# First attention of a two-block kernel: one head at a time against groups of four heads with 32-row score products

## What is computed

```python
def rope(x, positions):            # half = 32
    return jnp.concatenate([x1 * cos - x2 * sin, x2 * cos + x1 * sin], axis=-1)

scores = jnp.einsum('bcqhgd,bckhd->bchgqk', q, k_band) * (hd ** -0.5)
scores = jnp.where(mask[None, :, None, None], scores, -jnp.inf)
m = jnp.maximum(jnp.max(scores, axis=-1), sink_l)
p = jnp.exp(scores - m[..., None])
denom = jnp.sum(p, axis=-1) + jnp.exp(sink_l - m)
out = jnp.einsum('bchgqk,bckhd->bcqhgd', p, v_band)
out = out / denom.transpose(0, 1, 4, 2, 3)[..., None]
return out.reshape(B, S, Hq * hd).astype(h.dtype) @ w_out
```

## Time and profile before

| | |
|---|---|
| median of three runs | 1099.14 us |
| profiled execution | 1102.06 us (span 1100.3 us) |
| TensorE matmul busy | 1010.5 us, 92% of the span |
| VectorE busy | 590.8 us, 54% |
| ScalarE busy | 502.1 us, 46% |
| mean granted TensorE clock | 0.955 |
| span between the first head's first transpose and the last product of (`aout`,0) | 395.9 to 487.7 us |

### The profile page before, as it was taken

The page is one execution under the profiler, slowest core; times in us unless marked ns, Lnnn a source line. Parts: engine busy times, 40 slices in busy tenths (PEclk is TensorE's granted clock), DMA queues, the critical chain, the costliest instruction groups (busy, mean ns, idle before and its releaser), DMA issues.

```text
span 1100.3 us, 14326 instructions
## 1 busy us (share of the span) xinstructions
PE 1010.5 (92%) x5201; PEld 843.0 (77%) x5201; DVE 590.8 (54%) x1133; ACT 502.1 (46%) x834; POOL 24.4 (2%) x39
## 2 busy tenths in 40 slices
PE   3999898999999788997999999886899999999996
PEld 3976686888887777776888888775898888788875
DVE  4654766453543764347453544465554366565565
ACT  4555444353451665436343443356333444444542
POOL 0013100000000000000000000000000000000000
PEclk9999998999998987689999999988999999999999
DMA  6451145535444231024546455132242233433441
GB/s 247 173 202 38 68 170 192 206 142 224 164 179 152 78 115 39 1 77 164 212 157 229 147 196 201 66 116 96 83 168 77 77 115 122 147 115 120 149 172 39
DMA packets 25188, 149.46 MB, mean 136 GB/s; under 512 B 2960, under 2 KB 3088, under 8 KB 10800
## 3 DMA queue, kind: packets, MB, share of 16 engines
q1 hardware_dynamic: 24464, 146.39, 36.1%
q0 software_dynamic: 672, 2.38, 0.7%
HBM read 147.71 MB, written 1.05 MB: 135 GB/s over the span
## 4 chain that ended last, share of the span: by engine, by line
PE 79%; DVE 8%; ACT 7%; issue 2%; DVEq 2%; DMA 1%; ACTq 0%; SPq 0%
PE bank L414 22%; PE bank L415 22%; PE bank L416 22%; PE bank L473 2%; PE bank L742 1%; PE bank L719 1%; ACT w_hi L1033 1%; DVE w_lo L1464 1%; DVE w_lo L1485 1%; DVEq L1765 1%; PE bank L830 1%; ACT arena L1015 1%; PE bank L637 1%; PE bank L729 1%; PE bank L845 1%
## 5 line engine op out<-in xcount | busy, mean ns | idle before, releaser
L414 PE MATMUL bank<-w_hi,x_hi 128*128 128x512 f32 (+2 forms) x728 | 298.6, 410 | 14.7 <-DVE ffn_nat L1671 9.3
L415 PE MATMUL bank<-w_lo,x_hi 128*128 128x512 f32 (+2 forms) x728 | 289.9, 398 | 0.0
L416 PE MATMUL bank<-w_hi,x_lo 128*128 128x512 f32 (+2 forms) x728 | 287.4, 395 | 0.0
L414 PEld LDWEIGHTS bank<-w_hi,x_hi 128*128 128x128 f32 x728 | 140.1, 192 | 47.4 <-DVE w_lo L1464 10.1
L1404 DVE TENSOR_TENSOR w_lo<-w_raw,w_hi 128x2048 fp32r<-128x2048 f32 x62 | 140.2, 2288 | 60.1 <-ACT w_hi L978 57.4
L416 PEld LDWEIGHTS bank<-w_hi,x_lo 128*128 128x128 f32 x728 | 139.4, 192 | 31.4
L415 PEld LDWEIGHTS bank<-w_lo,x_hi 128*128 128x128 f32 x728 | 139.9, 192 | 25.9
L978 ACT ACTIVATE w_hi<-w_raw 128x2048 fp32r<-128x2048 f32 x60 | 112.9, 1909 | 31.1 <-DMA w_raw<-w_main_dram 26.6
L1485 DVE TENSOR_TENSOR w_lo<-w_raw,w_hi 128x2048 fp32r<-128x2048 f32 x38 | 86.9, 2290 | 54.7 <-ACT w_hi L1033 54.5
L1221 ACT ACTIVATE arena<-arena,small 128x144 f32<-128x144 f32 (+1 forms) x96 | 45.5, 474 | 111.2 <-DVE small L1768 96.7
L1671 DVE SCALAR_TENSOR_TENSOR ffn_nat<-bank,stat,ffn_nat 128x256 f32<-128x256 f32 x44 | 21.1, 483 | 132.5 <-ACT ffn_nat L1141 132.5
(11 more groups left out here) (284 smaller groups left out, 1452.8 us busy)
## 6 DMA issues: line engine op xcount, KB each, us to landing
w_raw<-w_main_dram SPq DMA_DIRECT2D x112, 1024.0 KB, 4.9
s_raw<-w_side_dram SPq DMA_DIRECT2D x51, 512.0 KB, 4.1
h<-x_dram SPq DMA_DIRECT2D x1, 1024.0 KB, 4.9
arena<-rows_dram POOLq DMA_DIRECT2D x2, 512.0 KB, 4.2
out_dram<-arena SPq DMA_DIRECT2D x1, 512.0 KB, 2.7
out_dram<-arena SPq DMA_DIRECT2D x2, 256.0 KB, 2.1
arena<-c_l_dram POOLq DMA_DIRECT2D x1, 384.0 KB, 5.4
arena<-c_b_dram POOLq DMA_DIRECT2D x1, 264.0 KB, 2.9
```

Source lines behind the costliest of these rows:

```text
L414: pe.matmul(out, ah, bh, start=first, stop=False)
L415: pe.matmul(out, ah, bl, start=False, stop=False)
L416: return pe.matmul(out, al, bh, start=False, stop=last)
```

## The change

- **Groups.** The 16 heads are taken in four groups of four. A group has one head of each key/value head; `HEADS` is reordered. Within a tile of 128 partitions lie now the first rotary halves (32 features) of four heads, and in a second tile their second halves. `aqT` is `[group, half, token]`.
- **Scores.** `a_scores(j)` does a group: for each 128 queries and each half, four products of 32 rows, one for each head, in its own 32 partitions and its own bank; the two halves add up in the bank. That is 16 products of 256 columns a group, where four heads had 8.
- **Rotation.** Both halves of a block pair come out in one bank (512 columns). VectorE multiplies by cos and by sin and adds across the two tiles; ScalarE's copies are gone.
- **Value and key projections.** `av` and `ak` are each one bank, and both are made inside the stream of transposes.
- **Order.** Masks, maxima and divisions go by group (`group_masked`, `group_attended`, one division of 512 columns), the sinks' exponentials once a group. ScalarE is three heads ahead of the transposes. Half blocks of the later queries stand between groups; the output's transposes and the first 6 of 8 steps of (`aout`,0) are inside the last group.
- **Meta tokens.** Their normalisation goes into `ffn(0)`, right behind the angles; their transposes behind the last head.

```diff
+NG = 4
-    keys += [("av", r) for r in range(R)] + [("ak", b) for b in range(2)]
-    keys += [("aq", b) for b in range(8)]
+    keys += [("av",), ("ak",)] + [("aq", j) for j in range(NG)]
...
-AQ_RIDERS = (1, 4, 7, 10)
-AOUT_SPLITS = (1, 4)
+A_HALVES = {0: (C_AOUT, 0), 4: (C_AOUT, 1), 9: (C_AOUT + 1, 0)}
...
-        sc_bank, o_bank = (bank[4], bank[3]), (bank[7], bank[2])
+        sc_bank, as_bank = (bank[4], bank[3]), (bank[2], bank[3], bank[4], bank[6])
...
+            def a_scores(j):
+
+                pe.wait_ge(rot_ok, 2 + j)
+                if j:
+                    pe.wait_ge(nm_ok, NG * j)
+                for r in range(R):
+                    for e in range(2):
+                        for g in range(NG):
+                            rows_ = slice(32 * g, 32 * g + 32)
+                            ins = pe.matmul(as_bank[g][:, r * S:(r + 1) * S], aqT[rows_, j, e, r * P:(r + 1) * P],
+                                            akT[rows_, e, :], start=(e == 0), stop=(e == 1))
+                            if (r, e) == (1, 1):
+                                ins.then_inc(sc_ps, 1)
...
+            a_scores(0)
+            a_queries(2, 0, KT // 2)
+            for j in range(NG):
+                n = NG * j
+                a_turn(n)
+                if j:
+                    a_values(n - 1)
+                if j < NG - 1:
+                    a_scores(j + 1)
+                if j < 2:
+                    a_queries(2 + j, (1 - j) * KT // 2, (2 - j) * KT // 2)
+                if j == NG - 1:
+                    a_out_turn(0)
+                    a_out_turn(1)
+                for i in range(1, NG):
+                    a_turn(n + i)
+                    a_values(n + i - 1)
+                    if (j, i) == (1, 1):
+                        a_queries(3, KT // 2, KT)
+                    if j == NG - 1 and i < NG - 1:
+                        for k in (2 * i - 2, 2 * i - 1):
+                            a_out_turn(k + 2)
+                            a_out_tiles(k)
+            a_out_tiles(KT - 4)
+            a_values(NH - 1)
+            a_out_tiles(KT - 3)
+            a_out_turn(KT - 2)
+            a_out_turn(KT - 1)
...
+                if layer == 0:
+                    act.wait_ge(meta_landed, 16)
+                    act.activation(um[0:M, :], hm[0:M, :], ACT.Square, accum_out=stat[0:M, 0:1]).then_inc(ss_ok, 1)
...
+            for n in range(NG - 1):
+                a_exps(n)
+            for n in range(NH):
+                act.wait_ge(pt_ps, n + 1)
+                if n >= 2:
+                    act.wait_ge(o_ps, n - 1)
+                act.activation(a_pt[:, n % 2, :, :], bank[5][:, :].rearrange("p (a b) -> p a b", a=4), ACT.Copy).then_inc(pt_ok, 1)
+                if n + NG - 1 < NH:
+                    a_exps(n + NG - 1)
+                if n in A_HALVES:
+                    c, g = A_HALVES[n]
+                    split_half(c, c % 2, g)
...
                 if layer == 0:
                     angles()
+                    rstd("meta", [(1, D)], rows=M, out=28)
+                    dve.tensor_scalar(um[0:M, :], hm[0:M, :], stat[0:M, 28:29], None, ALU.mult).then_inc(um_ok, 1)
...
+            def rotated(key, out):
+
+                b = acc_in(key)
+                both = b[:, :].rearrange("p (e s) -> p e s", e=2)
+                dve.drain()
+                dve.tensor_tensor(a_cos, both, cos2, ALU.mult)
+                dve.tensor_tensor(a_sin, both, sin2, ALU.mult).then_inc(acc_free[USE[key] % 2], 1)
+                dve.drain()
+                for e in range(2):
+                    ins = dve.tensor_tensor(out[:, e, :], a_cos[:, e, :], a_sin[:, 1 - e, :], ALU.add)
+                ins.then_inc(rot_ok, 1)
...
             ffn(0, x1)
+            rotated(("aq", 0), aqT[:, 0, :, :])
+            for g in range(2):
+                rest_half(C_AQ + 1, (C_AQ + 1) % 2, g)
+            rotated(("aq", 1), aqT[:, 1, :, :])
...
+            group_masked(0)
+            for j in range(NG):
+                if j:
+                    group_attended(j - 1)
+                if j < NG - 1:
+                    group_masked(j + 1)
+                if j < 2:
+                    rest_half(C_AOUT, C_AOUT % 2, j)
+                    rotated(("aq", 2 + j), aqT[:, 2 + j, :, :])
+                elif j == 2:
+                    rest_half(C_AOUT + 1, (C_AOUT + 1) % 2, 0)
+            rest_st("a_out", x_tile(x_hi), x_tile(x_lo), ks=range(4))
+            rest_half(C_AOUT + 1, (C_AOUT + 1) % 2, 1)
+            rest_st("a_out", x_tile(x_hi), x_tile(x_lo), ks=(4, 5))
+            group_attended(NG - 1)
+            rest_st("a_out", x_tile(x_hi), x_tile(x_lo), ks=(6, 7))
```

More of the change, by code:

```diff
@@ L766, in _, with a_out_turn, a_out_tiles @@
-            mixer_out("aout", C_AOUT, "a_out", lambda r, k: a_o[:, r, k * P:(k + 1) * P], {0: NH}, "f1", o_ok)
+            def a_out_turn(k):
+                if k == 0:
+                    pe.wait_ge(nm_ok, NH)
+                if k % 2 == 0:
+                    pe.wait_ge(o_ok, 2 * k + NG)
+                to_stationary("a_out", lambda r, k: a_o[:, r, k * P:(k + 1) * P], None, 0, ks=(k,))
+            def a_out_tiles(k):
+                st_wait("a_out", k)
+                for r in range(R):
+                    part_a(C_AOUT, ("aout", 0, r), r, k, k + 1)
@@ L767, in _ @@
+            a_out_tiles(KT - 4)
[3 more added lines that the diff above has]
+            a_out_turn(KT - 1)
+            pe.wait_ge(um_ok, 1)
+            for k in range(KT):
+                ins = pe.transpose(bank[6][:, k * M:(k + 1) * M], um[0:M, k * P:(k + 1) * P], ident[0:M, 0:M])
+            ins.then_inc(um_ps, 1)
+            a_out_tiles(KT - 2)
+            a_out_tiles(KT - 1)
+            mixer_rest("aout", C_AOUT, "f1")
             ffn(1, "aout")
@@ L1246, in _ @@
+            act.wait_ge(um_g, 1)
+            act.activation(x_hi[:, :, 0:M], m_tmp, ACT.Copy).then_inc(um_hi, 1)
             mixer_out("aout", C_AOUT, "f1", "norm_ffn1")
@@ L1431, in rest_st, with rstd @@
                     ins.then_inc(st_lo_ok, 1)
-            def rstd(name, parts, rows=P, first=0):
+            def rstd(name, parts, rows=P, first=0, out=24):
                 i, n = RMS[name], sum(w for w, _ in parts)
@@ L1450, in rstd @@
                     dve.drain()
-                    dve.scalar_tensor_tensor(out=y if step < 2 else stat[0:rows, 24:24 + n], in0=t, scalar=1.5, in1=y,
+                    dve.scalar_tensor_tensor(out=y if step < 2 else stat[0:rows, out:out + n], in0=t, scalar=1.5, in1=y,
                                              op0=ALU.add, op1=ALU.mult)
@@ L2059, in main_chunks @@
     return np.stack([k_tiles(p).reshape(P, 2, 4 * CH).transpose(1, 0, 2) for p in parts])
-HEADS = [8 * g + j + 4 * e for g in range(2) for j in range(4) for e in range(2)]
+HEADS = [4 * g + j for j in range(NG) for g in range(NG)]
 def side_units(i):
```

257 lines of the change are left out of this document (116 added, 141 removed).

## The result

The changed kernel takes 1062.61 us (median of 4 runs, 1060.24 to 1064.76) against 1099.80 for the kernel before (4 runs, 1098.64 to 1103.35). The ratio is 0.966, 95% interval 0.963 to 0.969: 37 us faster.

What follows compares the result with a forecast made beforehand. TensorE was taken as the bound, much of its head work at half clock. A gain of 23.3 us up to (`aout`,0), plus 2.0 behind it, less 3.3 in `ffn(0)`, made 22.0: from 1099.14 to 1077.1 us, range 1065 to 1090.

Steps and rivals of the forecast that it cites:

- Four side by side: Head scores: four 32-row products run at once, so a group's scores cost 2.1 us at full clock.
- none side by side: slower than before: Rival for the scores: 32-row products run one behind another, 8.5 us a group at full clock; 1101 to 1118, chance 0.05.
- Up to the first transposes: Attention's start: first head's transposes at 391.2 instead of 395.9, fourth mask ends at 393.0, about 3 us idle.
- The work from 393.0 on: TensorE's work from the second group's scores to the last product of (`aout`,0): 49.8 us at full clock.
- The factor 1.515: Head stretch: the old kernel's 91.8 us over 60.6 of full-clock work, for half clock and waits; applied, it gives 75.4 us.
- The first rival, the clock holds: Head stretch: dense halves and output products keep 2.4 GHz except some 7 us at the start; 1067 us, chance 0.12.
- The 4 us for dense products at the end: Last heads: output products fill 3.5 us of idle and should lift the clock earlier; 4 us taken off.
- Third weight half uncovered: Third group: ScalarE's split of a weight half, 1.91 us, lies under no riding products and would cost up to 1.9.
- Behind (`aout`,0): After that block's last product: the next chunk's load starts earlier, so the following transposes move up; 2 us gained.
- `ffn(0)`: First SwiGLU: the meta tokens' chain moved there makes TensorE wait 3.3 us more, a loss.
- Masks bound: Rival for the groups: both later groups' scores also wait 4.0 us for four masks; 1085 us, chance 0.08.

Runs made afterwards that it cites:

- e2: The changed kernel with a group's scores issued two heads at a time instead of four; 1070.76 us, ratio 0.976 to the kernel before.
- e1: The changed kernel with every group's scores issued one head after another, nothing side by side; 1107.05 us, ratio 1.009 to the kernel before.
- e12: The changed kernel with only the third and fourth groups' scores issued one head after another; 1083.23 us, ratio 0.987 to the kernel before.
- e9: The changed kernel plus 51 throwaway full-array products behind the scores of the third and of the fourth group; 1073.85 us, ratio 0.979 to the kernel before.
- e3: The changed kernel with the first six steps of (`aout`,0) moved behind the last head; 1064.42 us, ratio 0.970 to the kernel before.
- e11: The changed kernel with the meta chain later in the first SwiGLU and two weight halves moved; 1051.86 us, ratio 0.961 to the kernel before.
- e8: The changed kernel with the last two query pairs whole before the first head, not in halves between groups; 1067.38 us, ratio 0.976 to the kernel before.
- e13: The changed kernel with 51 throwaway full-array products at each of two places, each piece cut in four by waits; 1074.95 us, ratio 0.983 to the kernel before.
- e4: The changed kernel with the half query block before the first head moved behind the second group's scores; 1068.08 us, ratio 0.973 to the kernel before.

## Why the prediction was too high

- **Four side by side: right.** 2.1 us a group, measured 1.94. e2 gives 4.08 (4.2 by the prices of the text) and e1 11.9 x 0.65 = 7.7 of work at full clock (8.5). The rival "none side by side: slower than before" gave 1101 to 1118; e1 is 1107.
- **Up to the first transposes: right.** 391.2 and 393.0; measured 391.28 and 393.20, though the axis should have carried 3.3 us from `ffn(0)`. It carries 0.46: TensorE's first transposes of this attention start at 360.15, before at 359.69. The rest came back in places that the change does not touch, where this execution had less half clock; from 75 to 79 us the clock was 0.57 before and 1.00 after. So the piece in between took some 0.4 us less than forecast. That the clock would fall in the 3 us of waits here was wrong: the waits are 1.54 and 1.26, the clock 1.00.
- **The work from 393.0 on: right.** 49.8 at full clock forecast, 51.88 x 0.97 = 50.3 measured.
- **The factor 1.515: this step failed.** It carried half clock and waits over from before to a stretch with other work in it. 75.4 less 4 is 71.4 us; it took 54.2, a factor of 1.09. Those 17.2 us are more than the whole miss of 14.5. The changed kernel pays 27.1 us for a low clock when its thin scores run one after another (e1) and 1.7 when they run side by side. Thin scores took 22.5 us before; the change removes two thirds of that time, and the clock with which everything beside them runs goes up. The cause cannot be scaled with the total: e12 adds 12 us of thin work and pays 20.6, e9 adds as much dense work and pays 11.2.
- **The first rival, the clock holds,** had a chance of 0.12. By the prediction's own sign (a mean clock of the head stretch above 0.85; it is 0.97) it is the true one, and its price was too high: 61.5 us for the stretch, since it kept 8.2 of waits and 3.5 for a low clock at the start; measured are 2.3 and 1.6. Of the two reasons it gave, dense output products are not needed (e3). Dense halves between the groups did not have to be there either in e11's stretch of heads alone; taking both pairs out cost time in e8, but there waits came with it. What made the clock hold, the scores side by side, it did not name.
- **The 4 us for dense products at the end: wrong place.** e3 shows nothing clear of noise for where they stand (1.8 by medians).
- **Third weight half uncovered: right.** Up to 1.9 us; ScalarE's timeline in the changed kernel shows the split (L1094) ahead of the copy (L1293) for which TensorE waits 1.82 us, and the only half clock among the heads begins 2 us behind:

```profile
421.42 1.90 ACT L1094 ACTIVATE w_hi<-w_raw 128x2048 fp32r<-128x2048 f32 x1
423.22 0.57 ACT L1293 ACTIVATE arena<-bank 128x512 f32<-128x512 f32 x1
```

- **Behind (`aout`,0): right.** 2.0 forecast; 15.6 us before (487.7 to 503.31), 13.5 after (447.2 to 460.70), 2.1.
- **`ffn(0)`: nearly.** 3.3 forecast, 2.79 measured.
- **Masks bound: no,** only the second group's scores wait for masks (1.26 us), as in the sum; later scores wait 0.2 us in all, for a rotation (L1787).

In all, of 37.2 us by medians 22.0 were forecast. The profiled pair is 41.8 us apart, so 4.6 of its difference is the choice of executions. The gains of work, start and end were right to about 1 us each; the clock was not treated as something that the change sets.

**Open.** Whether it is the few rows, or the kind of operand and the time per row of results, that makes a product thin for the clock was not separated: the fillers of e9 are split products at twice the pace of the plain fp32 scores, and 64-row products alone were not put against 32-row products of equal length. The half-clock pieces outside the heads are not the same in every profile (75 to 79 us above), and the mean clock of one kernel differs between its executions; no run here looked at why. It is part of the spread, 5 us for the changed kernel and up to 16 for the kernel before.

## What to carry to other kernels

Price a stretch as work at full clock plus clock plus waits, and ask of each of the last two what in the stretch causes it before carrying it over: if the change removes the cause, the factor goes too. Score products of 32 rows are worth packing side by side twice over, for their own time and for the clock of the dense work beside them. But give them as many banks as run together, and check that the engines behind them can feed what TensorE now gains, or it waits for those instead: the pairs of 64-row products gained next to nothing here. A change that relies on overlap should be run once without it: here that version was slower than the kernel before.

## What the runs showed of the hardware that was not expected

- Four products of 32 rows in four partition quarters and four banks run side by side in plain fp32: 32 records in 1.94 us, against 4.08 in pairs and 7.7 of work one head after another (11.9 us at a mean clock of 0.65).
- The granted clock fell while the profile has TensorE 98% busy with thin products: 0.61 to 0.76 in e1's four stretches of 32-row products. With 12 us of full-array products added it stayed at 1.00 (e9), with e1's short waits between them too (e13).
- Once down, it stayed down through heads' transposes and values in which the profile has no gap (e12, 440.30 to 455.00, 0.50). Such heads kept a clock of 1.00 where it had not fallen (e11, 414.00 to 424.00).
- A wait of 4.55 us was followed by 6 us at half clock (e4), and a wait of 1.8 us among heads by about 3 (changed kernel, e9); waits of 1.54 and 1.26 us with a few products between them were not.
